# Pair products of the gated recurrence made within 64-token halves

## Chip, cores and metric

The kernel runs on one core of a Trainium2 chip. The metric is the device time of one execution in microseconds (us), smaller is better. Five engines work side by side, each through its own list of instructions in order: PE (TensorE, the matrix engine), DVE (VectorE), ACT (ScalarE), POOL (GpSimd) and SP, which issues DMAs here. They meet only at semaphores.

## What is computed

Two transformer blocks over 256 tokens of width 1024, all in float32. The change touches one part of the second block, a gated linear recurrence with 4 heads of key width 128 and value width 128:

```python
def hgrn2_mix(q, f_logit, i, g, lb, out_gain):
    ...
    def step(S, inp):
        qc, kc, vc, gc = inp
        b = jnp.cumsum(gc, axis=2)
        o_inter = jnp.einsum('bhck,bhkv->bhcv', qc * jnp.exp(b), S)
        diff = b[:, :, :, None, :] - b[:, :, None, :, :]
        decay = jnp.exp(jnp.where(causal[:, :, None], diff, -jnp.inf))
        A = jnp.einsum('bhtk,bhtsk,bhsk->bhts', qc, decay, kc)
        o = o_inter + jnp.einsum('bhts,bhsv->bhtv', A, vc)
        ...
        return S, o
```

The weight A of query t and key s (s not after t) is a sum over the 128 key channels of q, k and the product of all gates between s and t. Around it the second block has a sparse attention that picks 64 of 256 keys by index scores (heads 16 to 19 in the kernel), an attention over a memory (heads 20 to 23), and the projections and the feed-forward part, which make up most of the time.

## The kernel before

**The large products.** Every float32 weight is split by ACT into a high part (`whi`, line 817) and by DVE or POOL into the rest (`wlo`, lines 1177 and 1642), and every product is made as three matmuls (lines 470 to 472). Weights come in chunks of 256 rows through four buffers.

**The recurrence.** It is not run in steps. For each of 8 units u (head h = u // 2, tile of 128 tokens t = u % 2) the kernel makes A in blocks. The decay between key s and query t is split at a midpoint between them, so that it becomes a factor on k times a factor on q. There are 7 levels (`LEVELS`) of midpoints: level 0 splits the 128 tokens into two halves of 64, level 1 each half into quarters, and so on to neighbours; the diagonal, without decay, is the eighth. One unit goes through these steps:

1. "decay u": PE sums the log gates up to the midpoints (line 696, banks 0 and 1), and ACT takes their exponentials into `dec` (line 1119) in two pieces.
2. DVE makes `qd`, q times the factors of all 7 levels (line 1507), and for odd u `qx` (line 1512); POOL makes `kd` (line 1653), and for even u `kx`.
3. "pairs u": PE multiplies for each of the 7 levels and for the diagonal the whole 128 keys with the whole 128 queries (line 709): 8 products of 128x128, four into PSUM bank 2 and four into bank 3. For odd u one more product, "cross h" in bank 0, has the weights between the two tiles (line 713).
4. "weights u": DVE multiplies both banks by 0/1 masks that leave of each level the blocks that belong to it (line 1521, once for each bank, which also frees the bank), and sums the 8 levels into `AT` (line 1527). For odd u ACT copies the cross weights into `AT` (line 1147), which frees bank 0.
5. "hout h": PE multiplies `AT` with the values (lines 721 to 723) after the second unit of a head.

**What sets the order.** The list `MIX2`, written by hand, has all steps of this stage: gemm parts, units of the recurrence, index scores, rounds of "best" (the search of the largest index scores, lines 1485 and 1489) and attention heads ("scores", "probs", "pv"). Every engine walks through the same list and does its share of each entry, in order. So an instruction that waits holds up all later ones of its engine. The last pieces of it that matter here are

```python
("gemm", "sviq", 1), ("hout", 0), ("pairs", 2), ("decay", 3), ("sums", "sviq"),
("gemm", "mq", 0), ("turn", "iq"), *[("index", h) for h in range(4)], ("pairs", 3), ("decay", 4),
...
("gemm", "hg", 0), ("probs", 21), ("hout", 2), ("pairs", 6), ("pv", 21), ("decay", 7),
("scores", 22), ("divide", 22), ("best", 4), ("best", 5), ("turn", "sqk"), ("scores", 23), ("divide", 23),
("gemm", "hg", 1), ("pairs", 7), ("probs", 22), ("pv", 22), ("probs", 23), ("pv", 23), ("hout", 3),
```

**PSUM banks.** Banks 0 to 3 are shared by all small steps. A step claims a bank, which waits until the step before it in that bank has been read out. Banks 0 and 1 hold decays, cross, hout, index and scores; bank 2 pairs and transposed probabilities (line 544, copied out at line 908), bank 3 pairs and the attention outputs ("pv", lines 556 and 558, copied out at line 914).

Of the kernel before, what the change touches and what calls it, by code (L numbers as in the profile page):

```python
# [24 lines left out]
AX = mybir.AxisListType  # L25
# [36 lines left out]
C_HEND = C_HM + 8 * P  # L62


def constants():
# [9 lines left out]
    for n in range(LEVELS):  # L75
# [6 lines left out]
        g[:, C_HM + n * P:C_HM + (n + 1) * P] = same & late & (s <= mid)  # L82
    g[:, C_HC + 8 * P:C_HC + 9 * P] = s <= t
    g[:, C_HM + 7 * P:C_HM + 8 * P] = s == t
# [122 lines left out]
def program(nc, dram, out, known):  # L207
# [12 lines left out]
    with ctx:  # L220
# [68 lines left out]
        masked = sb("masked", [P, 8, P], where=a3)  # L289
        kx, qx = sb("kx", [P, P], where=a3), sb("qx", [P, P], where=a3)  # L290
# [147 lines left out]
        def _(pe):  # L438
# [260 lines left out]
            def hgrn_pairs(u):  # L699
# [4 lines left out]
                for b in range(2):  # L704
                    claim(2 + b, f"pairs {u}")
                    for c in range(4):
                        n, ts = 4 * b + c, slice(t * P, (t + 1) * P)
                        k, q = (kd[:, n, :], qd[:, n, :]) if n < LEVELS else (hkT[:, h, ts], hqT[:, h, ts])
                        mm = nc.tensor.matmul(X[2 + b][:, c * P:(c + 1) * P], k, q, start=True, stop=True)  # L709
                    full(mm, 2 + b, f"pairs {u}")  # L710
# [91 lines left out]
        def _(act):  # L802
# [320 lines left out]
            for kind, n, *rest in MIX2:  # L1123
# [18 lines left out]
                elif kind == "pairs" and n % 2 == 1:  # L1142
                    h = n // 2
                    act.wait_ge(*at("bank0 full", f"cross {h}"))
                    if h:
                        act.wait_ge(*at("bank1 full", f"hout {h - 1}"))
                    done(A(AT[:, 2, :], X[0][:, 0:P], ACT.Copy), "bank0 free", f"cross {h}")
# [21 lines left out]
        def _(dve):  # L1169
# [331 lines left out]
            def q_decayed(u):  # L1501
                h, t = u // 2, u % 2
                dve.wait_ge(*at("bank1 free", f"decay {u}"))
                if u:
                    dve.wait_ge(*at("bank3 full", f"pairs {u - 1}"))
# [9 lines left out]
            def weights(u):  # L1515

                h, t = u // 2, u % 2
                dve.wait_ge(*(at("weights summed", f"{u - 1}") if u else at("hgrn q", "0")))
                for b in range(2):
                    dve.wait_ge(*at(f"bank{2 + b} full", f"pairs {u}"))  # L1520
                    done(V.tensor_tensor(masked[:, 4 * b:4 * b + 4, :], X[2 + b].rearrange("p (l s) -> p l s", s=P),
                                         hgc[:, C_HM + b * 512:C_HM + (b + 1) * 512].rearrange("p (l s) -> p l s", s=P),
                                         ALU.mult), f"bank{2 + b} free", f"pairs {u}")
                dve.wait_ge(*at("bank3 free", f"pairs {u}"))
                if h:
                    dve.wait_ge(*at("bank1 full", f"hout {h - 1}"))
# [84 lines left out]
        def _(pool):  # L1611
# [23 lines left out]
            for kind, n, *rest in MIX2:  # L1635
# [10 lines left out]
                elif kind == "decay":  # L1646
# [3 lines left out]
                    if u:  # L1650
                        pool.wait_ge(*at("bank3 full", f"pairs {u - 1}"))
# [44 lines left out]
```

## Time and profile before

| what | value |
|---|---|
| three runs | 877.44, 881.36 and 881.86 us, median 881.36 |
| profiled execution, first to last instruction | 877.9 us |
| its own time beside the span | not listed apart from the three runs; one of them is 0.5 us below the span |
| instructions | 10694 |
| PE busy | 806.9 us, 92% |
| DVE busy | 550.7 us, 63% |
| ACT busy | 485.0 us, 55% |
| POOL busy | 85.5 us, 10% |
| stage of the recurrence | about 505 to 636 us of the span |

Busy shares are means over the whole program. In a row of a view "x14" says that 14 instructions are put together, and the words behind "<-" in square brackets say what ended the idle time before the first of them. A float32 matmul shows as two PE instructions. PE means the matmul itself, PEld the load of its stationary operand, 128*64 a stationary operand of 128 rows and 64 columns.

### The profile page before, as it was taken

The numbers are of one execution on the slowest core, as the hardware profiler recorded it, in microseconds if no ns is written. First come the engines' busy times: TensorE is split into PE (matmuls) and PEld (weight loads), VectorE is DVE, ScalarE is ACT, GpSimd is POOL, SyncE is SP. The second block draws the span as 40 slices with busy tenths as digits, with TensorE's granted clock in tenths as the row PEclk, the third lists the DMA queues.
The fourth block names the chain that finished last, engine by engine and source line by source line (L and its number), as shares of the span: only waits on it lengthen the run. The fifth ranks groups of instructions, "written<-read, shape, count | busy, mean of one in ns | idle before, by whom it ended". The sixth has DMA issues, their size and how long they took to land.

```text
span 877.9 us, 10694 instructions
## 1 busy us (share of the span) xinstructions
PE 806.9 (92%) x3811; PEld 650.4 (74%) x3811; DVE 550.7 (63%) x814; ACT 485.0 (55%) x739; POOL 85.5 (10%) x50
## 2 busy tenths in 40 slices
PE   4979999999799999999999798797849999999998
PEld 3767787777578888888888667665636878888886
DVE  5676565566736877777472666788773666665650
ACT  4755554666326777776254744433542677777630
POOL 0022000000000000000000047463222000000000
PEclk9999988999999999999999989898969999999999
DMA  8765153234307755545384533231001675555550
GB/s 293 296 209 173 49 162 126 96 97 143 121 24 219 238 191 190 182 151 179 134 269 164 171 95 110 70 97 49 24 25 49 198 236 179 185 181 170 194 166 24
DMA packets 70566, 130.21 MB, mean 148 GB/s; under 512 B 6558, under 2 KB 13046, under 8 KB 70142
## 3 DMA queue, kind: packets, MB, share of 16 engines
q1 hardware_dynamic: 69662, 124.90, 44.0%
q10 hardware_dynamic: 864, 4.78, 1.4%
q8 instruction: 25, 0.41, 0.2%
q14 instruction: 15, 0.12, 0.0%
HBM read 128.61 MB, written 1.05 MB: 148 GB/s over the span
## 4 chain that ended last, share of the span: by engine, by line
PE 71%; DVE 11%; ACT 8%; DMA 5%; issue 3%; POOL 1%; SPq 1%; ACTq 0%; DVEq 0%; POOLq 0%
PE acc L470 20%; PE acc L472 19%; PE acc L471 19%; DVE b_wlo L1177 3%; DMA b_raw<-in_w_in 2%; PE banks L531 2%; PE banks L696 2%; PE banks L571 2%; ACT b_whi L817 2%; PE banks L556 2%; PE banks L709 1%; DMA b_raw<-in_w_mem_kv 1%; DMA b_raw<-in_w_ffn_in 1%; PE banks L544 1%; PE banks L513 1%
## 5 line engine op out<-in xcount | busy, mean ns | idle before, releaser
L1177 DVE TENSOR_TENSOR b_wlo<-b_raw,b_whi 128x1024 fp32r<-128x1024 f32 (+3 forms) x222 | 253.4, 1179 | 103.1 <-ACT b_whi L817 101.4
L817 ACT ACTIVATE b_whi<-b_raw 128x1024 fp32r<-128x1024 f32 (+3 forms) x244 | 234.2, 1001 | 76.5 <-DMA b_raw<-in_w_in 19.1
L470 PE MATMUL acc<-b_whi,b_hhi 128*128 128x512 f32 (+3 forms) x528 | 207.7, 393 | 8.8 <-DVE b_hlo L1448 4.6
L472 PE MATMUL acc<-b_wlo,b_hhi 128*128 128x512 f32 (+3 forms) x528 | 200.4, 380 | 0.0
L471 PE MATMUL acc<-b_whi,b_hlo 128*128 128x512 f32 (+3 forms) x528 | 200.4, 380 | 0.0
L470 PEld LDWEIGHTS acc<-b_whi,b_hhi 128*128 128x128 f32 x528 | 102.3, 194 | 31.9 <-DVE b_hlo L1448 5.1
L471 PEld LDWEIGHTS acc<-b_whi,b_hlo 128*128 128x128 f32 x528 | 102.4, 194 | 18.2 <-issue 1.5
L472 PEld LDWEIGHTS acc<-b_wlo,b_hhi 128*128 128x128 f32 x528 | 102.0, 193 | 18.5
L470 PE MATMUL acc<-b_whi,b_ohi 128*128 128x512 f32 (+1 forms) x272 | 106.0, 390 | 6.1 <-DVE b_wlo L1177 2.9
L471 PE MATMUL acc<-b_whi,b_olo 128*128 128x512 f32 (+1 forms) x272 | 103.6, 381 | 0.0
L472 PE MATMUL acc<-b_wlo,b_ohi 128*128 128x512 f32 (+1 forms) x272 | 103.5, 381 | 0.0
L472 PE MATMUL acc<-b_wlo,b_ahi 128*128 128x512 f32 x176 | 69.1, 393 | 0.0
L470 PE MATMUL acc<-b_whi,b_ahi 128*128 128x512 f32 x176 | 69.1, 393 | 0.0
L471 PE MATMUL acc<-b_whi,b_alo 128*128 128x512 f32 x176 | 68.7, 390 | 0.0
L1653 POOL TENSOR_TENSOR b_kd<-b_dec,b_hkT 128x896 f32<-128x896 f32 x8 | 21.4, 2670 | 463.5 <-ACT b_dec L1119 463.5
L470 PEld LDWEIGHTS acc<-b_whi,b_ohi 128*128 128x128 f32 x272 | 51.8, 190 | 17.0 <-DVE b_wlo L1177 3.3
L472 PEld LDWEIGHTS acc<-b_wlo,b_ohi 128*128 128x128 f32 x272 | 51.7, 190 | 9.8
L471 PEld LDWEIGHTS acc<-b_whi,b_olo 128*128 128x128 f32 x272 | 51.8, 191 | 8.9
L1642 POOL TENSOR_TENSOR b_wlo<-b_raw,b_whi 128x1024 fp32r<-128x1024 f32 (+1 forms) x22 | 49.2, 2252 | 59.8 <-ACT b_whi L817 59.8
L471 PEld LDWEIGHTS acc<-b_whi,b_alo 128*128 128x128 f32 x176 | 33.1, 188 | 7.3
L472 PEld LDWEIGHTS acc<-b_wlo,b_ahi 128*128 128x128 f32 x176 | 33.1, 188 | 7.2
L470 PEld LDWEIGHTS acc<-b_whi,b_ahi 128*128 128x128 f32 x176 | 33.1, 188 | 6.9
(213 smaller groups left out, 909.5 us busy)
## 6 DMA issues: line engine op xcount, KB each, us to landing
b_raw<-in_w_in SPq DMA_DIRECT2D x64, 512.0 KB, 4.6
b_raw<-in_w_ffn_up SPq DMA_DIRECT2D x40, 512.0 KB, 4.7
b_raw<-in_w_ffn_in SPq DMA_DIRECT2D x40, 512.0 KB, 4.6
b_raw<-in_w_ffn_down SPq DMA_DIRECT2D x22, 512.0 KB, 5.6
b_raw<-in_w_ffn_out SPq DMA_DIRECT2D x22, 512.0 KB, 4.5
b_raw<-in_w_out SPq DMA_DIRECT2D x16, 512.0 KB, 3.7
b_raw<-in_w_mem_kv SPq DMA_DIRECT2D x4, 512.0 KB, 9.8
b_gates<-in_b_gate ACTq DMA_DIRECT2D x2, 1024.0 KB, 8.3
```

Source lines behind the costliest of these rows:

```text
L470: nc.tensor.matmul(o, a, wh, start=first, stop=False)
L471: nc.tensor.matmul(o, b, wh, start=False, stop=False)
L472: mm = nc.tensor.matmul(o, a, wl, start=False, stop=last)
L513: mm = nc.tensor.transpose(X[bank][:, c * S + t * P:c * S + (t + 1) * P], src[:, t, cols], ident)
L531: mm = nc.tensor.matmul(X[b][:, c0:c1], q[:, t * P:(t + 1) * P], k[:, 0:c1 - c0], start=True, stop=not fox)
L556: nc.tensor.matmul(o[:, 0:S], v[:, 0, :], pt[:, 0:S], start=True, stop=False)
L571: mm = nc.tensor.transpose(X[base + b][:, c * S + t * P:c * S + (t + 1) * P], src[:, t, (2 * b + c) * P:(2 * b + c + 1) * P], ident)
L696: full(nc.tensor.matmul(X[b][:, :], logf[:, t, h * P:(h + 1) * P], hgc[:, c:c + 512], start=True, stop=True), b, f"decay {u}")
L817: A(whi[:, n % SPLIT, 0:c["nk"], 0:c["n"]], raw[:, n % RAW, 0:c["nk"], 0:c["n"]], ACT.Copy)\
L1177: V.tensor_tensor(wlo[:, n % SPLIT, 0:c["nk"], 0:c["n"]], raw[:, n % RAW, 0:c["nk"], 0:c["n"]], whi[:, n % SPLIT, 0:c["nk"], 0:c["n"]].bit ...
L1642: G.tensor_tensor(wlo[:, low % SPLIT, 0:c["nk"], 0:c["n"]], raw[:, low % RAW, 0:c["nk"], 0:c["n"]], whi[:, low % SPLIT, 0:c["nk"], 0:c["n" ...
L1653: ins = G.tensor_tensor(kd[:, :, :], dec[:, 1 - t:8 - t, :], k.unsqueeze(1).to_broadcast([P, LEVELS, P]), ALU.mult)
```

## The change

The masks of levels 1 to 6 and of the diagonal leave nothing outside the two diagonal 64x64 blocks; level 0 alone has the block of keys 0 to 63 and queries 64 to 127, and fills it. The change makes just these blocks. Level 1 to 6 and the diagonal are two 64x64 products each, the first half of the tokens to partitions 0 to 63 and the second to partitions 64 to 127, in 7 x 64 = 448 columns of bank 2; level 0 is one 64x64 product in the last 64 columns of bank 2, on partitions 0 to 63. Bank 3 is no longer used by pairs. DVE multiplies 448 columns by masks and sums 7 levels into a new tile `near` (64 columns). ACT copies three 64x64 blocks into `AT`: level 0 out of the bank, which now is what frees bank 2, and after the sum the two blocks of `near`. The fourth block of `AT` is set to zero once. What waited for "weights summed" in "hout" now waits for "weights placed".

```diff
+def by_half(m):
+    return np.concatenate([m[:64, :64], m[64:, 64:]])
...
+        near = sb("near", [P, 64], where=a3)
...
-                for b in range(2):
-                    claim(2 + b, f"pairs {u}")
-                    for c in range(4):
-                        n, ts = 4 * b + c, slice(t * P, (t + 1) * P)
-                        k, q = (kd[:, n, :], qd[:, n, :]) if n < LEVELS else (hkT[:, h, ts], hqT[:, h, ts])
-                        mm = nc.tensor.matmul(X[2 + b][:, c * P:(c + 1) * P], k, q, start=True, stop=True)
-                    full(mm, 2 + b, f"pairs {u}")
+                claim(2, f"pairs {u}")
+                for n in range(1, LEVELS + 1):
+                    for r in range(2):
+                        own, ts = slice(64 * r, 64 * r + 64), slice(t * P + 64 * r, t * P + 64 * r + 64)
+                        k, q = (kd[:, n, own], qd[:, n, own]) if n < LEVELS else (hkT[:, h, ts], hqT[:, h, ts])
+                        nc.tensor.matmul(X[2][own, (n - 1) * 64:n * 64], k, q, start=True, stop=True)
+                full(nc.tensor.matmul(X[2][0:64, LEVELS * 64:512], kd[:, 0, 0:64], qd[:, 0, 64:P], start=True, stop=True),
+                     2, f"pairs {u}")
...
-                pe.wait_ge(*at("weights summed", f"{2 * h + 1}"))
+                pe.wait_ge(*at("weights placed", f"{2 * h + 1}"))
...
-                elif kind == "pairs" and n % 2 == 1:
-                    h = n // 2
-                    act.wait_ge(*at("bank0 full", f"cross {h}"))
+                elif kind == "pairs":
+                    h, t = n // 2, n % 2
                     if h:
                         act.wait_ge(*at("bank1 full", f"hout {h - 1}"))
-                    done(A(AT[:, 2, :], X[0][:, 0:P], ACT.Copy), "bank0 free", f"cross {h}")
+                    act.wait_ge(*at("pairs masked", f"{n}"))
+                    done(A(AT[0:64, t, 64:P], X[2][0:64, LEVELS * 64:512], ACT.Copy), "bank2 free", f"pairs {n}")
+                    if t == 1:
+                        act.wait_ge(*at("bank0 full", f"cross {h}"))
+                        done(A(AT[:, 2, :], X[0][:, 0:P], ACT.Copy), "bank0 free", f"cross {h}")
+                    act.wait_ge(*at("weights summed", f"{n}"))
+                    A(AT[0:64, t, 0:64], near[0:64, :], ACT.Copy)
+                    done(A(AT[64:P, t, 64:P], near[64:P, :], ACT.Copy), "weights placed", f"{n}")
...
-                for b in range(2):
-                    dve.wait_ge(*at(f"bank{2 + b} full", f"pairs {u}"))
-                    done(V.tensor_tensor(masked[:, 4 * b:4 * b + 4, :], X[2 + b].rearrange("p (l s) -> p l s", s=P),
-                                         hgc[:, C_HM + b * 512:C_HM + (b + 1) * 512].rearrange("p (l s) -> p l s", s=P),
-                                         ALU.mult), f"bank{2 + b} free", f"pairs {u}")
-                dve.wait_ge(*at("bank3 free", f"pairs {u}"))
-                if h:
-                    dve.wait_ge(*at("bank1 full", f"hout {h - 1}"))
-                done(V.tensor_reduce(AT[:, t, :], masked.rearrange("p l s -> p s l"), AX.X, ALU.add),
+                dve.wait_ge(*at("bank2 full", f"pairs {u}"))
+                n = LEVELS * 64
+                part = masked.rearrange("p l s -> p (l s)")[:, 0:n]
+                done(V.tensor_tensor(part, X[2][:, 0:n], hgc[:, C_HM:C_HM + n], ALU.mult), "pairs masked", f"{u}")
+                dve.wait_ge(*at("pairs masked", f"{u}"))
+                if u:
+                    dve.wait_ge(*at("weights placed", f"{u - 1}"))
+                done(V.tensor_reduce(near[:, :], part.rearrange("p (l s) -> p s l", s=64), AX.X, ALU.add),
                      "weights summed", f"{u}")
...
+            V.memset(AT[64:P, 0:2, 0:64], 0.0)
```

The table `hgc` with the masks shrinks from 2176 to 1600 columns (one DMA). Where DVE and POOL waited for "bank3 full" of the unit before, they wait for "bank2 full".

ACT around unit 2, before: between the splits of the weights and the exponentials of decay 3 nothing stands for an even unit.

```order
L817 ACTIVATE b_whi<-b_raw 128x1024 [waits s_chunk_used,s_raw_3_in]
L1119 ACTIVATE b_dec<-banks 128x512 [waits s_bank0_full,s_k_decayed,s_q_decayed]
L1119 ACTIVATE b_dec<-banks 128x512 [waits s_bank1_full]
L848 ACTIVATE b_sv<-acc,b_rs 128x256 [waits s_tile_0_summed]
L848 ACTIVATE b_spare<-acc,b_rs 128x256
```

The same place in the change:

```order
L825 ACTIVATE b_whi<-b_raw 128x1024 [waits s_chunk_used,s_raw_3_in]
L1155 ACTIVATE b_AT<-banks 64x64 [waits s_pairs_masked,s_bank1_full]
L1160 ACTIVATE b_AT<-b_near 64x64 [waits s_weights_summed]
L1161 ACTIVATE b_AT<-b_near 64x64
L1127 ACTIVATE b_dec<-banks 128x512 [waits s_bank0_full,s_k_decayed,s_q_decayed]
L1127 ACTIVATE b_dec<-banks 128x512 [waits s_bank1_full]
L856 ACTIVATE b_sv<-acc,b_rs 128x256 [waits s_tile_0_summed]
L856 ACTIVATE b_spare<-acc,b_rs 128x256
```

Three copies that wait for DVE now stand ahead of the exponentials.

PE around unit 6, before: pairs 6, then the attention output of head 21 (lines 556 and 558), then decay 7.

```order
L709 MATMUL banks<-b_qd,b_kd 128x128 [waits s_bank2_free,s_k_decayed,s_q_decayed]
L709 MATMUL banks<-b_qd,b_kd 128x128 x3
L709 MATMUL banks<-b_qd,b_kd 128x128 [waits s_bank3_free]
L709 MATMUL banks<-b_qd,b_kd 128x128 x2
L709 MATMUL banks<-b_hqT,b_hkT 128x128
L556 MATMUL banks<-b_spare,b_mv 64x256 [waits s_bank3_free,s_bank2_free]
L558 MATMUL banks<-b_spare,b_mv 64x256
L696 MATMUL banks<-b_hgc,b_logf 128x512 [waits s_bank0_free,s_log_f]
```

The same place in the change:

```order
L716 MATMUL banks<-b_qd,b_kd 64x64 [waits s_bank2_free,s_k_decayed,s_q_decayed]
L716 MATMUL banks<-b_qd,b_kd 64x64 x11
L716 MATMUL banks<-b_hqT,b_hkT 64x64 x2
L717 MATMUL banks<-b_qd,b_kd 64x64
L563 MATMUL banks<-b_spare,b_mv 64x256 [waits s_bank3_free,s_bank2_free]
L565 MATMUL banks<-b_spare,b_mv 64x256
L703 MATMUL banks<-b_hgc,b_logf 128x512 [waits s_bank0_free,s_log_f]
```

The attention output still waits for bank 3, which pairs 6 filled before and doesn't now.

## Rows read from the trace of the kernel before

**Rows 1.** Busy time by stretch: us, each engine's busy us, PE clock granted, DMA.
```profile
core 0: us, PE busy (x) PEld busy (x) DVE busy (x) ACT busy (x) POOL busy (x), PEclk, DMA share, GB/s
520.00:540.00 20.00, 19.54 (x104) 15.65 (x103) 12.72 (x12) 7.94 (x20) 13.59 (x8) 1.00 0.32 86
...
560.00:580.00 20.00, 15.34 (x69) 11.95 (x70) 17.44 (x26) 6.54 (x13) 9.60 (x4) 0.83 0.33 106
580.00:600.00 20.00, 16.63 (x83) 12.43 (x81) 16.21 (x44) 10.53 (x23) 8.53 (x5) 1.00 0.16 52
600.00:620.00 20.00, 16.13 (x61) 11.39 (x62) 15.68 (x23) 4.39 (x11) 8.29 (x3) 0.83 0.18 53
```

**Rows 2.** Chain that ended last, 505 to 640: start us, us, what.
```profile
537.26 1.73 PE banks L696 x4
539.13 0.38 issue
539.51 0.47 ACT b_sv L848
...
543.94 0.28 ACT b_ikT L1134
544.26 0.71 PE banks L672 x4
...
605.77 0.41 DVE b_xn L1588
606.18 1.21 DVE b_masked L1521 x2
607.52 0.80 PE banks L556 x2
```

**Rows 3.** DVE groups of mask and sum: busy us, mean ns, idle before.
```profile
L1527 DVE TENSOR_REDUCE b_AT<-b_masked 128x128 f32<-128x1024 f32 x8 | 15.5, 1938 | 0.3
L1521 DVE TENSOR_TENSOR b_masked<-banks,b_hgc 128x512 f32<-128x512 f32 x16 | 10.8, 687 | 4.1 <-PE banks L709 3.4
```

**Rows 4.** PE in order of time, units 1 and 4.
```profile
524.76 1.72 PE L709 MATMUL banks<-b_qd,b_kd 128*128 128x128 f32 x14
527.39 1.96 PE L696 MATMUL banks<-b_hgc,b_logf 128*128 128x512 f32 x4 [0.46 <-ACT b_AT L1147]
...
571.53 1.72 PE L709 MATMUL banks<-b_qd,b_kd 128*128 128x128 f32 x14
573.31 1.88 PE L696 MATMUL banks<-b_hgc,b_logf 128*128 128x512 f32 x4
```

**Rows 5.** PE in order of time: 128x8 products, and a change to 64 columns.
```profile
119.95 0.25 PE L470 MATMUL acc<-b_whi,b_hhi 128*128 128x8 f32 x1
120.06 0.25 PE L471 MATMUL acc<-b_whi,b_hlo 128*128 128x8 f32 x1
...
139.35 0.49 PE L544 MATMUL banks<-b_cst,b_Sm 128*128 128x128 f32 x3
139.78 0.43 PE L556 MATMUL banks<-b_PT,b_v 128*64 128x256 f32 x1
```

**Rows 6.** PEld by tile: ns min/median/max of loads with 128 and 64 columns.
```profile
L709 PEld LDWEIGHTS banks<-b_qd,b_kd x112: 186/192/338, 515.7 to 622.1; 128*128 128x128 f32 x112
...
L556 PEld LDWEIGHTS banks<-b_kd,b_sv x8: 133/136/227, 650.4 to 670.7; 128*64 128x64 f32 x8
```

**Rows 7.** PE in order of time, index scores 0 and 1 on two halves of the rows.
```profile
544.26 0.71 PE L672 MATMUL banks<-b_ikT,b_spare 64*128 64x256 f32 x4 [1.32 <-ACT b_ikT L1134]
544.80 0.39 PE L673 MATMUL banks<-b_ikT,b_spare 64*128 64x128 f32 x4
```

**Rows 8.** ACT in order of time: a 128x8 step, then decay 5.
```profile
567.43 0.21 ACT L828 ACTIVATE b_rs<-b_ms 128x8 f32<-128x8 f32 x1 [2.19 <-DVE b_ms L1251]
...
574.46 0.60 ACT L1119 ACTIVATE b_dec<-banks 128x512 f32<-128x512 f32 x1 [4.68 <-PE banks L696]
```

**Rows 9.** DVE in order of time, unit 4 and unit 6.
```profile
572.69 1.52 DVE L1521 TENSOR_TENSOR b_masked<-banks,b_hgc 128x512 f32<-128x512 f32 x2 [0.68 <-PE banks L709]
...
606.10 1.27 DVE L1521 TENSOR_TENSOR b_masked<-banks,b_hgc 128x512 f32<-128x512 f32 x2
...
612.80 1.09 DVE L1507 TENSOR_TENSOR b_qd<-b_dec,b_hqT 128x896 f32<-128x896 f32 x1 [2.75 <-ACT b_dec L1119]
```

**Rows 10.** ACT in order of time, unit 7 (and its copy of the cross weights).
```profile
624.94 0.27 ACT L1147 ACTIVATE b_AT<-banks 128x128 f32<-128x128 f32 x1
625.35 0.60 ACT L908 ACTIVATE b_spare<-banks 128x512 f32<-128x512 f32 x1
```

**Rows 11.** PE in order of time, units 6 and 7.
```profile
607.52 0.80 PE L556 MATMUL banks<-b_spare,b_mv 128*64 128x256 f32 x2 [2.90 <-DVE b_masked L1521]
...
624.66 0.66 PE L544 MATMUL banks<-b_cst,b_spare 128*128 128x128 f32 x4 [1.71 <-DVE b_masked L1521]
```

More of the change, by code:

```diff
@@ L61 @@
 C_HM = C_HC + 9 * P
-C_HEND = C_HM + 8 * P
+C_HEND = C_HM + LEVELS * 64
+def by_half(m):
+    return np.concatenate([m[:64, :64], m[64:, 64:]])
 def constants():
@@ L81, in constants @@
         same = s // (2 * half) == t // (2 * half)
-        g[:, C_HM + n * P:C_HM + (n + 1) * P] = same & late & (s <= mid)
+        if n:
+            g[:, C_HM + (n - 1) * 64:C_HM + n * 64] = by_half(same & late & (s <= mid))
     g[:, C_HC + 8 * P:C_HC + 9 * P] = s <= t
-    g[:, C_HM + 7 * P:C_HM + 8 * P] = s == t
+    g[:, C_HM + (LEVELS - 1) * 64:C_HM + LEVELS * 64] = by_half(s == t)
     freq = (500000.0 ** (-np.arange(8) * 2.0 / 16)).astype(np.float32)
@@ L1504, in q_decayed @@
                 if u:
-                    dve.wait_ge(*at("bank3 full", f"pairs {u - 1}"))
+                    dve.wait_ge(*at("bank2 full", f"pairs {u - 1}"))
                 q = hqT[:, h, t * P:(t + 1) * P]
@@ L1515, in weights @@
             def weights(u):
-                h, t = u // 2, u % 2
                 dve.wait_ge(*(at("weights summed", f"{u - 1}") if u else at("hgrn q", "0")))
-                for b in range(2):
-                    dve.wait_ge(*at(f"bank{2 + b} full", f"pairs {u}"))
-                    done(V.tensor_tensor(masked[:, 4 * b:4 * b + 4, :], X[2 + b].rearrange("p (l s) -> p l s", s=P),
-                                         hgc[:, C_HM + b * 512:C_HM + (b + 1) * 512].rearrange("p (l s) -> p l s", s=P),
-                                         ALU.mult), f"bank{2 + b} free", f"pairs {u}")
-                dve.wait_ge(*at("bank3 free", f"pairs {u}"))
-                if h:
-                    dve.wait_ge(*at("bank1 full", f"hout {h - 1}"))
-                done(V.tensor_reduce(AT[:, t, :], masked.rearrange("p l s -> p s l"), AX.X, ALU.add),
+                dve.wait_ge(*at("bank2 full", f"pairs {u}"))
[6 more added lines that the diff above has]
+                done(V.tensor_reduce(near[:, :], part.rearrange("p (l s) -> p s l", s=64), AX.X, ALU.add),
                      "weights summed", f"{u}")
@@ L1650, in _ @@
                     if u:
-                        pool.wait_ge(*at("bank3 full", f"pairs {u - 1}"))
+                        pool.wait_ge(*at("bank2 full", f"pairs {u - 1}"))
                     k = hkT[:, h, t * P:(t + 1) * P]
```

## Prediction

> **What bounds the kernel now.** I read busy time by stretch first, then the chain that ended last through the stage of the recurrence, then DVE's groups, then each engine in order of time around single units. Outside 505 to 636 us the change touches nothing but one DMA of a table, so all of the answer lies in these 130 us. There PE is busy 19.5 of 20 us up to 540 and 15 to 17 of 20 behind 560, where DVE is busy 16 to 17 of 20 [rows 1]. Neither is the bound alone: both walk one hand-written list, and the chain passes from PE to ACT and DVE and back. At unit 2 it goes PE decay, ACT copies of the projections, ACT `ikT`, PE index scores [rows 2]; at unit 6 it goes DVE copy, DVE mask, PE attention output of head 21 [rows 2]. So DVE time saved counts where DVE is on that chain, and ACT time added counts where ACT is.
>
> **What goes: DVE work.** Mask and sum cost 2 x 0.69 + 1.94 = 3.3 us a unit [rows 3]. Scaled by columns, the new ones cost 0.687 x 448 / 512 = 0.60 us and 1.938 x 448 / 1024 = 0.85 us; the sum takes out 64 columns of 7 where it took 128 of 8, which scales alike. That is 1.5 us a unit, 1.8 us less, 15 us over 8 units. Most of it isn't on the chain: in units 0 to 5 DVE waits behind it for ACT's next exponentials.
>
> **PE's burst.** Before, 16 instructions of pairs run 111 ns apart, 1.78 us (571.53 to 573.31) [rows 4]. Now there are 15 products, 30 instructions. No row has 64 stationary and 64 moving columns at once. Matmuls of 8 moving columns with a 128-column load also come 111 ns apart [rows 5], so there the load sets the distance; loads of 64 columns take 136 ns against 192, 56 ns less for 64 columns [rows 6]. One after the other, 56 ns each, 30 take 1.7 us. The change to a 64-column operand puts 0.21 us between starts where 0.11 is usual (the third of line 544 starts 139.57, line 556 at 139.78) [rows 5], twice a unit: 1.9 us. From the other side, the index scores on two halves of the rows overlap: four starts of 256 columns lie within 0.33 us, and all eight starts within 0.66 us [rows 7], where 111 ns per 128 columns gives 1.3 us. If the two halves of columns overlap fully, 30 instructions take 0.84 + 0.2 = 1.05 us. The nearest row on overlap is of rows, not columns, so I take the middle, 1.5 us, called B. The upper end is that nothing gets shorter: 30 x 0.111 + 0.2 = 3.5 us.
> The Trainium skill (TensorEngine Tiling, Key Properties) says that tiles work independently, loads and matmuls in parallel, and that a change of the tiling mode drains TensorE. By this page alone B would be near 1.05 us, and the sum 2.7 us lower than mine; rows 7 agree for tiles of rows, and no row here shows it for columns.
>
> **The new path of a unit.** Before, DVE starts on bank 2 at 1.16 us after the first matmul (572.69 against 571.53) [rows 4, 9], 0.38 us behind the start of the eighth, while the rest still runs. Now the mask waits for all 30, so it starts at B + 0.33. Then the mask takes 0.62 with its hand-over, the sum 0.86. ACT: a copy of 128x128 is 0.27 us [rows 10] and a 128x8 step is 0.21 [rows 8], so a 64x64 copy is about 0.22, with hand-over 0.25. The marks from the first matmul on:
> - bank 2 free: B + 0.33 + 0.62 + 0.3 = B + 1.25 = 2.75 us
> - cross copied, and PE's decay on its way: B + 1.63 = 3.13 us
> - ACT through with both copies of `near`, and at the exponentials: B + 0.33 + 0.62 + 0.9 + 0.5 = B + 2.35 = 3.85 us
>
> **Unit by unit.**
> - Unit 0: ACT comes to decay 1 at 3.85 us instead of some 3.0; DVE's `qd` was held up by its own sum, so only 0.35 us is left, and PE had 0.2 us of its own work to cover it. PE's shorter burst is lost in that wait. +0.2.
> - Units 1 and 3: decay u+1 needs bank 0, and waits for ACT's copy of the cross weights: 527.39 - 524.76 = 2.63 us before [rows 4], 3.13 now. Behind it PE has gemms and is on the chain. 2 x 0.5 = +1.0.
> - Units 2 and 4: ACT is at the exponentials 2.93 us after the first matmul (574.46 against 571.53) [rows 4, 8]; at 3.85 it is 0.9 late, of which 0.18 comes back since its second piece has no wait left. The chain runs through ACT here (`sv`, `ikT` for the index scores in unit 2 [rows 2], the transposed memory queries in unit 4). 2 x 0.75 = +1.5.
> - Unit 5: transposed probabilities need bank 2, free at 2.75, then decay 6 follows, 0.6 later than before. +0.6.
> - Unit 6, the one gain: PE's output of head 21 waits 2.90 us for DVE's mask to free bank 3 [rows 11], behind it decay 7, and DVE's `qd` waits 2.75 us for that [rows 9]. In the change nothing of pairs lies in bank 3, so PE runs on. What is left is DVE and ACT: mask from 606.10 [rows 9], + 0.65 + 0.86 = 607.6, copies of `near` to 608.1, ACT's copy of the output to 608.5, exponentials 1.15 to 609.65, `qd` at 609.7 instead of 612.80. From there DVE is the chain. -3.1.
> - Unit 7: probabilities of head 22 need bank 2. Before, the first mask freed it, and PE started at 624.66 [rows 11]. Now ACT must copy level 0, and ACT splits weights until 624.94 [rows 10]: PE starts at 625.25, and ACT's copy behind it comes after the copies of `near`, 0.6 late. +0.6. DVE's saving of 1.8 us is of no use, the next DVE step waits for ACT.
> - At nothing: the zeroing of a block, once, where DVE waits for ACT's splits; the table DMA, hidden by gemms before decay 0; the issue of 14 more matmul instructions a unit, inside B. Uncovered, the zeroing and the DMA cost at most some tenths of a microsecond, once.
>
> Sum: 0.2 + 1.0 + 1.5 + 0.6 - 3.1 + 0.6 = +0.8 us. Against the profiled span that is 877.9 to 878.7; the span is 3.5 us below the median of the three runs, and I add the same difference to the median: 881.4 + 0.8 = 882.2 us. B enters in six places: B = 1.05 gives -1.9 us, 1.9 gives +3.2, 3.5 gives +12.8.
>
> **Rivals.**
> 1. *Small matmuls cost as much as large ones* (slower). If issue or a fixed part and not the columns sets the 111 ns, B is 3.5 us. For it: 8 moving columns were no faster than 128 [rows 5]. Against: the loads with 64 columns are shorter [rows 6]. It decides from B = 2.2 on, where the sum passes +4.4 us. Time 894 us. Chance 0.12.
> 2. *ACT's waits hold up the splits* (slower). ACT now stands behind DVE's sum in each unit, and the weight splits behind it. If one chunk in each of units 4 to 7 came late by the 1.5 us that the sum and copies take, +6 on top: 888 us. Against: ACT is idle more than half of this stage [rows 1]. Chance 0.08.
> 3. *DVE's relief counts in full* (faster). Units 4 to 7 lie where DVE is the busiest next to PE. If the 1.8 us counted in units 4, 5 and 7 too, and the columns overlapped, it is 0.8 - 2.7 - 3 x 1.8 = -7 us: 874 us. For it: DVE busy 16 to 17 of 20 us [rows 1]. Against: the waits above. Chance 0.15.
>
> **Numbers.** My forecast, the sum with B between 1.05 and 1.9, has 0.65: about 879 to 885 us. Some 0.5% (4.4 us) is what a measurement of this kernel can tell from no change, and the three runs spread by as much. Faster by more than that 0.15, within it 0.65, slower 0.20. The range has to take in a part of both other cases: 876 to 890 us.
>
> **What would show it.** The first 64x64 matmul and the following decay in an even unit tell B: 1.5 us forecast, 3.5 in rival 1. DVE's mask should be 0.60 us and its sum 0.85. ACT's copies 0.22. PE's idle time for DVE ahead of the output of head 21, 2.9 us, must be gone, and the index scores of unit 2's turn start about 1 to 2 us later than at 544.26. If the sum stays near 1.9 us, or B is over 2.2, the forecast is wrong on the slow side; if ACT reaches the exponentials as early as before, on the fast side.

## The result, and the profile after

The change takes 883.72 us (median of 20 runs, 877.79 to 888.23) against 878.65 us for the kernel before (20 runs), a ratio of 1.0054 with the interval 1.0034 to 1.0073. The same kernel beside the experiments gave 1.0032 (1.0005 to 1.0058). So it is slower by 3 to 5 us, just around the 0.5% that a measurement can tell. The forecast was 882.2 us and "no change"; the time lies in its range. The forecast of the difference was +0.8 us, on a baseline of 881.4 us from three runs; the median of 20 runs of the kernel before is 878.65, so 2.7 us of the agreement in time are that baseline. The medians and ratios below leave out two slow runs, one of "cross copy first" (887.84 us; with it the median is 881.75) and one of "DVE, sum twice" (1155.76 us).

The head of the page of the change. PE has 112 instructions more and 3 us more of busy time, DVE 17 us less, ACT 5.5 us more.

```profile
span 884.8 us, 10939 instructions
PE 809.9 (92%) x3923; PEld 648.1 (73%) x3923; DVE 533.8 (60%) x807; ACT 490.5 (55%) x763; POOL 87.3 (10%) x50
PEclk9999988999999999999999989798959999999999
```

The groups of the new work, by line: busy us, mean ns, idle before and who ended it. They answer to [rows 3].

```profile
L1539 DVE TENSOR_REDUCE b_near<-b_masked 128x64 f32<-128x448 f32 x8 | 7.4, 924 | 0.3
L1535 DVE TENSOR_TENSOR b_masked<-banks,b_hgc 128x448 f32<-128x448 f32 x8 | 5.0, 621 | 9.6 <-PE banks L717 9.6
L1155 ACT ACTIVATE b_AT<-banks 64x64 f32<-64x64 f32 x8 | 1.7, 217 | 29.6 <-DVE b_masked L1535 29.6
L1160 ACT ACTIVATE b_AT<-b_near 64x64 f32<-64x64 f32 x8 | 2.1, 256 | 4.6 <-DVE b_near L1539 4.6
```

Mask 0.62 us (forecast 0.60), sum 0.92 (0.85), ACT's copies 0.22 and 0.26 (0.22). PE in order of time at unit 4, the place of [rows 4]:

```profile
575.39 0.92 PE L716 MATMUL banks<-b_qd,b_kd 128*64 128x64 f32 x24
576.13 0.29 PE L716 MATMUL banks<-b_hqT,b_hkT 128*64 128x64 f32 x4
576.25 0.28 PE L717 MATMUL banks<-b_qd,b_kd 128*64 128x64 f32 x2
576.46 1.98 PE L703 MATMUL banks<-b_hgc,b_logf 128*128 128x512 f32 x4
579.54 0.63 PE L520 MATMUL banks<-b_cst,b_tokA 128*128 128x128 f32 x4 [1.09 <-ACT b_dec L1127]
```

From the first product to the decay sums behind it are 576.46 - 575.39 = 1.07 us for 30 instructions: B is 1.07, not 1.5. So the burst is 0.7 us shorter than before (1.78). PE does not get to keep it: the last row has a wait of 1.09 us that the kernel before doesn't have. The chain that ended last shows why. First the kernel before, at unit 4 (start us, us, what):

```profile
571.69 1.78 PE banks L709 x16
573.48 1.72 PE banks L696 x4
575.20 0.00 issue
575.20 0.64 PE banks L513 x4
```

It stays on PE. The same stretch of the change:

```profile
575.46 0.96 PE banks L716 x28
576.64 0.64 DVE b_masked L1535
577.30 0.93 DVE b_near L1539
578.80 0.60 ACT b_dec L1127
579.54 0.64 PE banks L520 x4
```

It leaves PE, goes through DVE's mask and sum and, between 578.23 and 578.80, through ACT's two copies of `near`, and comes back by the exponentials. Before, the sum was no part of this chain: nothing but `qd` of the next unit stood behind it. The copies stand ahead of the exponentials in ACT's list, so DVE's sum now holds up PE, though it has become shorter.

**Where PE's time went**, from the start of pairs u to the start of pairs u + 1 (the last line to the output of head 3), us. "Gemm" is how much longer the gemm part in that stretch took; its 24 instructions are the same in both kernels. "Rest" is the difference without it.

| from | before | change | difference | gemm | rest | forecast |
|---|---|---|---|---|---|---|
| pairs 0 | 9.05 | 8.44 | -0.61 | | -0.61 | +0.2 |
| pairs 1 | 10.55 | 10.47 | -0.08 | | -0.08 | +0.5 |
| pairs 2 | 12.20 | 12.75 | +0.55 | | +0.55 | +0.75 |
| pairs 3 | 24.02 | 25.30 | +1.28 | +1.54 | -0.26 | +0.5 |
| pairs 4 | 11.63 | 13.81 | +2.18 | +1.70 | +0.48 | +0.75 |
| pairs 5 | 17.81 | 17.28 | -0.53 | | -0.53 | +0.6 |
| pairs 6 | 19.81 | 20.29 | +0.48 | +2.11 | -1.63 | -3.1 |
| pairs 7 | 8.58 | 7.42 | -1.16 | | -1.16 | +0.6 |
| sum | 113.65 | 115.76 | +2.11 | +5.35 | -3.24 | +0.8 |

The gemm column is a lower clock. Busy time by stretch of just these three parts (the counts take in neighbours at the edges), before:

```profile
core 0: us, PE busy (x) PEld busy (x) DVE busy (x) ACT busy (x) POOL busy (x), PEclk, DMA share, GB/s
565.20:571.50 6.30, 6.30 (x26) 5.20 (x26) 5.20 (x9) 2.35 (x5) 2.59 (x2) 0.87 0.01 5
577.60:583.20 5.60, 5.60 (x26) 4.64 (x26) 4.72 (x17) 0.81 (x3) 0.38 (x1) 1.00 0.01 3
615.20:620.80 5.60, 5.60 (x26) 4.63 (x26) 4.41 (x17) 2.00 (x6) 0.63 (x1) 1.00 0.00 0
```

and in the change:

```profile
567.50:575.40 7.90, 7.90 (x28) 6.07 (x27) 5.71 (x9) 2.38 (x5) 4.17 (x2) 0.70 0.07 18
581.90:589.20 7.30, 7.30 (x25) 5.58 (x25) 5.17 (x19) 2.85 (x6) 1.86 (x2) 0.77 0.00 0
619.10:626.80 7.70, 7.70 (x27) 5.93 (x26) 5.03 (x23) 4.22 (x12) 0.18 (x1) 0.72 0.01 2
```

PE is busy all the time in all six; the granted clock is 0.70 to 0.77 where it was 0.87 to 1.00. About half of each part runs at 1.2 GHz, the rest at 2.4. The rest column is not free of the clock either: behind pairs 6, 16 instructions of PE ahead of the gemm (scores and a turn) take 3.14 us before (612.06 to 615.20) and 4.29 in the change (614.79 to 619.08). The stage alone accounts for 2.1 us in this pair of traces; the rest of the 6.9 us between the spans lies ahead of it (decay 0 starts at 507.26 before, at 509.98 in the change) and behind it (2.1 us), where the code is the same. In the kernels below the part ahead took 503.0 to 512.6 us in one trace each, and no edit touches it. So I read stages from traces, and whole times from medians. A stage is one execution too: a second trace of the change, below, has 126.9 us for it where this one has 124.2.

### The profile page after: what moved, and what is told of

Its sections match the earlier page's. It is cut to its first block, busy times and chain, and to the rows that moved or that the text cites. A ratio compares the mean times of both kernels' runs of the same rounds, so it can differ in the third digit from the quotient of the medians.

```text
span 884.8 us, 10939 instructions
## 1 busy us (share of the span) xinstructions
PE 809.9 (92%) x3923; PEld 648.1 (73%) x3923; DVE 533.8 (60%) x807; ACT 490.5 (55%) x763; POOL 87.3 (10%) x50
## 3 DMA queue, kind: packets, MB, share of 16 engines
HBM read 128.32 MB, written 1.05 MB: 146 GB/s over the span
## 4 chain that ended last, share of the span: by engine, by line
PE 70%; DVE 11%; ACT 8%; DMA 6%; issue 3%; POOL 1%; SPq 1%; ACTq 0%; DVEq 0%; POOLq 0%
PE acc L477 20%; PE acc L479 19%; PE acc L478 19%; DVE b_wlo L1191 3%; PE banks L538 3%; ACT b_whi L825 2%; DMA b_raw<-in_w_in 2%; PE banks L578 2%; DMA b_raw<-in_w_ffn_up 2%; PE banks L563 1%; DMA b_raw<-in_w_mem_kv 1%; DMA b_raw<-in_w_ffn_in 1%; PE banks L703 1%; PE banks L520 1%; PE banks L551 1%
## 5 line engine op out<-in xcount | busy, mean ns | idle before, releaser
L477 PE MATMUL acc<-b_whi,b_hhi 128*128 128x512 f32 (+3 forms) x528 | 210.3, 398 | 13.3 <-DVE b_wlo L1191 5.7
L478 PE MATMUL acc<-b_whi,b_hlo 128*128 128x512 f32 (+3 forms) x528 | 202.8, 384 | 0.0
L479 PE MATMUL acc<-b_wlo,b_hhi 128*128 128x512 f32 (+3 forms) x528 | 202.7, 384 | 0.0
L1666 POOL TENSOR_TENSOR b_kd<-b_dec,b_hkT 128x896 f32<-128x896 f32 x8 | 24.1, 3010 | 463.3 <-ACT b_dec L1127 463.3
```

What stands on the lines that cost most here:

```text
L477: nc.tensor.matmul(o, a, wh, start=first, stop=False)
L478: nc.tensor.matmul(o, b, wh, start=False, stop=False)
L479: mm = nc.tensor.matmul(o, a, wl, start=False, stop=last)
L1666: ins = G.tensor_tensor(kd[:, :, :], dec[:, 1 - t:8 - t, :], k.unsqueeze(1).to_broadcast([P, LEVELS, P]), ALU.mult)
```

## Experiments

Twelve experiments, two of them repeats. Ratios are to the kernel before on the same chip, with 95% intervals; 12 runs of each kernel below the first two rows. The groups ran on three chips, where the kernel before has medians of 879.65, 879.72 and 880.21 us.

| kernel | median, us | ratio | stage in its trace, decay 0 to head 3's output |
|---|---|---|---|
| before | 878.65 | 1 | 122.1 |
| change | 883.72 | 1.0054 (1.0034 to 1.0073) | 124.2 |
| change again | 882.22 | 1.0032 (1.0005 to 1.0058) | 126.9 |
| pad | 881.16 | 1.0019 (0.9986 to 1.0052) | 122.4 |
| pad and warm | 878.79 | 0.9998 (0.9974 to 1.0021) | 121.0 |
| all copies on DVE | 874.57 | 0.9940 (0.9909 to 0.9972) | 115.8 |
| the same again | 874.59 | 0.9937 (0.9910 to 0.9963) | 115.7 |
| near copies on DVE | 878.73 | 0.9994 (0.9972 to 1.0017) | 122.7 |
| level 0 copy on DVE | 882.70 | 1.0027 (0.9994 to 1.0059) | 126.0 |
| cross copy first | 880.51 | 1.0009 (0.9977 to 1.0041) | 126.4 |
| DVE, bank 3 held | 878.53 | 1.0001 (0.9978 to 1.0024) | 120.9 |
| DVE, products twice | 877.92 | 0.9982 (0.9957 to 1.0007) | 123.1 |
| DVE, sum twice | 877.78 | 0.9963 (0.9933 to 0.9994) | 120.2 |
| DVE and warm | 874.58 | 0.9934 (0.9903 to 0.9964) | 115.8 |

### Is it the clock? The change again, padded, and warmed

"Change again" is the change, unaltered.

> The change once more, unaltered, to see how much of the difference between two traces is the kernel's and how much one execution's. Both theories: a ratio of about 1.005 to the kernel before. If the clock is the cause, its executions with a lower mean granted clock are the longer ones, and the stretches in which a gemm runs at the lower clock are not the same as in the first trace; the burst of pairs must again be 1.05 us and the way to the exponentials 3.4 us.

In its trace the burst at unit 4 is again 1.07 us, and ACT is at the exponentials 580.86 - 577.45 = 3.41 us behind the first product, as in the first trace. The three gemm parts are long again, but not by the same amounts:

```profile
570.50:577.40 6.90, 6.90 (x26) 5.40 (x25) 5.71 (x9) 2.44 (x5) 3.11 (x2) 0.80 0.03 12
584.40:591.20 6.80, 6.80 (x25) 5.27 (x24) 4.73 (x19) 2.79 (x6) 1.35 (x2) 0.82 0.00 0
622.70:630.80 8.10, 8.10 (x26) 6.18 (x26) 4.61 (x21) 3.72 (x8) 2.12 (x1) 0.68 0.01 2
```

They add 4.2 us to the kernel before, and the stage is 4.8 us longer, so the rest is +0.6 us here where the first trace has -3.2. What both traces show can be built on; the sum of the rest column can't.

"Pad" puts four 128x128 products of constants, which nobody reads, into bank 3, which pairs no longer use, behind each unit's pairs. They add work for PE and nothing for anyone else.

```diff
+            def pad(step, k):
+                claim(3, step)
+                for c in range(k):
+                    mm = nc.tensor.matmul(X[3][:, c % 4 * P:(c % 4 + 1) * P], hgc[:, 0:P], hgc[:, P:2 * P], start=True, stop=True)
...
+                pad(f"pad {u}", 3)
```

> The change, and behind each unit's pairs (and cross) 4 more products of 128x128 on constants into bank 3, 0.9 us of TensorE work whose result nobody reads and for which nobody waits; it lies where TensorE waits for ScalarE or is ahead of it. Theory clock (the change leaves TensorE less busy, and it is granted the lower clock more often): mean clock up, time 2 to 5 us below the change's, back near the kernel before. Theory ScalarE (its copies and waits cost the time): no gain, 0 to 3 us longer than the change, as TensorE has 7 us more to do.

"Pad and warm" adds to these 18 such products ahead of the output of head 1 and 13 ahead of pairs 6, where PE waits 5.05 and 3.01 us.

> The padded kernel, and in the two long idle stretches of TensorE (5.1 us before the output of head 1, 3.0 us before pairs 6) 18 and 13 more products of 128x128 on constants, 4.0 and 2.9 us. Theory clock: the gemms behind both stretches run at the full clock from their start, mean clock over 0.965, time 3 to 7 us below the change's, below the kernel before too. Theory ScalarE: no gain over the padded kernel.

With only more work for PE the time fell: 882.2, 881.2, 878.8 us side by side. The first two agree within their intervals, the last lies 3.4 us below the change (the intervals still overlap). The mean granted clock of the 12 runs goes 0.957, 0.962, 0.969, and is 0.964 for the kernel before beside them. The same three gemm parts in the warmed kernel:

```profile
566.30:572.00 5.70, 5.70 (x27) 4.44 (x25) 4.98 (x11) 3.01 (x6) 2.05 (x1) 1.00 0.12 46
578.60:584.20 5.60, 5.60 (x25) 4.39 (x24) 4.48 (x17) 1.14 (x5) 1.06 (x1) 1.00 0.00 1
614.60:622.00 7.40, 7.40 (x27) 5.68 (x26) 4.76 (x22) 4.22 (x12) 0.18 (x1) 0.75 0.01 2
```

Two of three are back at 5.66 us and clock 1.00 (7.87 and 7.27 in the change); the third stayed at 0.75, though 13 products stand ahead of pairs 6, some 13 us before it. "Pad" alone has 6.50, 5.66 and 7.52 us. So the four products behind pairs 4 are enough for the second part, and the first took the 18 of the warmed kernel besides.

The second part is the one that ties the clock to a wait. Four products fill PE's wait of 1.09 us behind pairs 4 (0.22 us of it are left in "pad"). Over all the traces of this document the part sorts by that wait: where it is 1.09 to 1.28 us (the change twice, cross copy first, level 0 copy on DVE) the part took 6.77 to 8.15 us, and in the ten traces without it 5.57 to 5.69.

How much of the whole loss is the clock stays open. The three parts say 5.4 and 4.2 us in the two traces of the change. The 3.4 us of the warmed kernel are no measure of it, since the kernel before has the two filled waits as well (5.06 and 3.62 us), and was not padded itself. Over the 20 runs of the change a lower mean clock goes with a longer span, a straight line through them having 5 us a hundredth (885.4 and 886.4 us at 0.946, 875.9 and 876.4 at 0.961); that is no cause yet, as the warmed version of the best kernel shows below.

### Which copy? All three, two, one, and the order

"All copies on DVE" makes the three 64x64 copies on DVE, the first between mask and sum, and leaves ACT as in the kernel before.

```diff
+                done(V.tensor_copy(AT[0:64, t, 64:P], X[2][0:64, LEVELS * 64:512]), "bank2 free", f"pairs {u}")
...
+                V.tensor_copy(AT[0:64, t, 0:64], near[0:64, :])
+                done(V.tensor_copy(AT[64:P, t, 64:P], near[64:P, :]), "weights placed", f"{u}")
```

> The change with the three 64x64 copies of each unit made by VectorE in place of ScalarE (ScalarE's share is again that of before, one copy of the cross weights for odd units). Theory ScalarE: exponentials of even units start 2.3 us behind the first matmul of pairs and not 3.4, q decayed 0.9 us sooner, time 2 to 4 us below the change's. Theory clock: within 1.5 us of the change, TensorE being as idle as in it.

It is 0.6% faster than the kernel before and 0.9% than the change: 7.7 us, where I had expected 2 to 4. The repeat agrees to 0.02 us in the median and to 0.1 us in the stage.

> The run with all three copies on VectorE again, unaltered. If its gain is real, the ratio lies between 0.991 and 0.997 and the profiled run shows a PE wait of under 1 us before the decay sums of unit 4; a ratio over 0.999 would say that the first one was luck.

Its chain at unit 4 (the repeat) is on PE alone again, and 3.0 us long where before it was 3.5 (575.20 - 571.69):

```profile
564.77 0.97 PE banks L716 x28
565.73 0.11 PE banks L717 x2
565.84 1.91 PE banks L703 x4
567.75 0.00 issue
567.76 0.64 PE banks L520 x4
```

ACT is at the exponentials 567.01 - 564.70 = 2.31 us behind the first product, where the change needs 578.80 - 575.39 = 3.41 and the kernel before 2.93 [rows 4, 8].

"Near copies on DVE" moves only the two copies of `near` (with the waits that this needs); ACT keeps the level 0 copy.

> The change with only the two copies out of near moved to VectorE; ScalarE keeps the copy of level 0, which waits for the mask but not for the sum. Theory that the wait for the sum is the cost: exponentials of even units at 2.3 us again, time within 1.5 us of 874.6. Theory that any wait of ScalarE for VectorE costs it, unit 6 above all, where the mask comes late: 2 us or more above 874.6, between that and the change.

"Level 0 copy on DVE" is the other half.

> The change with the level 0 copy alone on VectorE (between mask and sum), the two near copies stay on ScalarE. It completes the square with the runs that moved the near copies alone and all three. Queue theory (what hurts is the level 0 copy ahead of the cross copy): no PE wait over 1 us before the decay sums of unit 4, and most of the gain of the run with all three: a ratio of about 0.996 to 0.998, 876 to 879 us. If the near copies ahead of the exponentials are the larger part, the ratio stays at 1.001 to 1.003 and the exponentials of unit 1 start still at 3.3 to 3.5 us behind the pairs' first product, where all three on VectorE gave 2.3.

"Cross copy first" moves nothing, it turns ACT's order round for the odd units.

```diff
+                    if t == 1:
+                        act.wait_ge(*at("bank0 full", f"cross {h}"))
+                        done(A(AT[:, 2, :], X[0][:, 0:P], ACT.Copy), "bank0 free", f"cross {h}")
                     act.wait_ge(*at("pairs masked", f"{n}"))
                     done(A(AT[0:64, t, 64:P], X[2][0:64, LEVELS * 64:512], ACT.Copy), "bank2 free", f"pairs {n}")
```

> The change with one thing altered: for the odd units ScalarE moves the cross product out of bank 0 before it waits for the mask and moves the level 0 product. Queue theory (the cross copy stands behind a copy that waits for VectorE's mask, so bank 0 comes free late and TensorE waits before the next unit's decay sums, above all in unit 3 where the mask waits behind the index sums): the wait of TensorE before the decay sums of unit 4 falls from 1.27 us to about 0.5, those of units 2 and 6 by 0.3 to 0.5 us, and the time is 1 to 3 us below the change (881 to 883). If the copies' load on ScalarE is the cost and not their order, the time stays at that of the change within 1 us, since nothing is taken off ScalarE.

My queue theory named the level 0 copy as the larger one, and its forecast failed. With that copy alone on DVE I expected most of the gain and got little of it (1.0027, forecast 0.996 to 0.998); in the medians the near copies alone are worth more (0.9994), and both together more than the two apart (0.994). The intervals allow either half to be the larger, and also a plain sum. PE's waits in the traces say what each copy does. Four of them grew in the change (us; "again" is the second trace of the same kernel):

| PE waits before | before | change | again | cross first | level 0 on DVE | near on DVE | all on DVE |
|---|---|---|---|---|---|---|---|
| index scores of unit 2's turn | 1.32 | 1.83 | 1.83 | 1.83 | 1.83 | 1.33 | 1.33 |
| decay sums of unit 2 | 0.46 | 0.87 | 0.87 | 0.46 | 0.46 | 0.87 | 0.46 |
| decay sums of unit 4 | 0.46 | 1.27 | 0.62 | 0.52 | 0.52 | 2.59 | 0.64 |
| the turn behind decay 5 | none | 1.09 | 1.10 | 1.10 | 1.28 | none | none |
| three gemm parts, length | 17.5 | 22.8 | 21.7 | 21.6 | 20.7 | 19.3 | 17.9 |

The first of these waits and the one behind decay 5 belong to the copies of `near`, which stand ahead of the exponentials; with the level 0 copy alone on DVE both stay. ACT in order of time there, unit 4:

```profile
572.00 0.26 ACT L1159 ACTIVATE b_AT<-b_near 64x64 f32<-64x64 f32 x1 [5.30 <-DVE b_near L1541]
572.26 0.25 ACT L1160 ACTIVATE b_AT<-b_near 64x64 f32<-64x64 f32 x1
572.54 1.09 ACT L1128 ACTIVATE b_dec<-banks 128x512 f32<-128x512 f32 x2
```

and PE:

```profile
573.28 0.63 PE L520 MATMUL banks<-b_cst,b_tokA 128*128 128x128 f32 x4 [1.28 <-ACT b_dec L1128]
```

The two waits before decay sums belong to the level 0 copy: it waits for the mask, and the cross copy, which frees the bank, stands behind it on ACT. In unit 1 that costs PE 0.41 us in each of the three traces of the table with that order and nothing in the others. In unit 3 the mask waits besides behind DVE's index sums, and the size varies from one execution to the next (1.27 and 0.62 us in the same kernel). With only the near copies on DVE it is at its worst, DVE, then ACT, then PE:

```profile
544.65 0.61 DVE L1533 TENSOR_TENSOR b_masked<-banks,b_hgc 128x448 f32<-128x448 f32 x1
545.36 0.22 ACT L1156 ACTIVATE b_AT<-banks 64x64 f32<-64x64 f32 x1 [1.74 <-DVE b_masked L1533]
545.48 0.26 ACT L1159 ACTIVATE b_AT<-banks 128x128 f32<-128x128 f32 x1
```

```profile
545.88 2.90 PE L703 MATMUL banks<-b_hgc,b_logf 128*128 128x512 f32 x3 [2.59 <-ACT b_AT L1159]
```

The cross product was in its bank at 543.3 and its copy needed nothing but ACT. In "cross copy first" the added wait before unit 2's decay sums is gone, as expected, and before unit 4's there are 0.52 us. Its ratio stands 2 us below the one of the change and 4 us below the other, its stage (126.4 us) is no shorter than those of the change, and the intervals overlap, so what the order alone is worth stays open. Each half of the move takes away one kind of wait and leaves the other, and in these traces the gemm parts stay long with either; the last row of the table has 5.3 and 4.2 us over the kernel before in the change, 0.4 with all copies on DVE. Against the mean ratio of the change, 1.0043, the near copies alone give -4.3 us, the level 0 copy alone -1.4, both -9. The medians carry these three numbers; the reading by waits and clock is from one trace each, two for the change and for all copies on DVE.

The copies are not always cheap on DVE. Of the 16 copies of `near` in the repeat's trace, 12 take 0.19 us; those of units 5 and 7 take 0.63 and 2.30, 1.03 and 2.30 us. Unit 5, DVE and then POOL:

```profile
579.35 2.30 DVE L1541 COPY b_AT<-b_near 64x64 f32<-64x64 f32 x1
576.92 4.67 POOL L1656 TENSOR_TENSOR b_wlo<-b_raw,b_whi 128x1024 fp32r<-128x1024 f32 x2 [5.44 <-ACT b_whi L825]
```

In both units each of the two copies ends within 0.07 us of the end of one of POOL's two instructions.

### What were bank 3, B and DVE's time worth?

All three start from "all copies on DVE". "Bank 3 held" puts the level 0 product back into bank 3, so that pairs hold two banks as in the kernel before.

```diff
-                full(nc.tensor.matmul(X[2][0:64, LEVELS * 64:512], kd[:, 0, 0:64], qd[:, 0, 64:P], start=True, stop=True),
-                     2, f"pairs {u}")
+                full(mm, 2, f"pairs {u}")
+                claim(3, f"pairs {u}")
+                full(nc.tensor.matmul(X[3][0:64, LEVELS * 64:512], kd[:, 0, 0:64], qd[:, 0, 64:P], start=True, stop=True),
+                     3, f"pairs {u}")
```

> The kernel with the copies on VectorE, with the product of level 0 put back into bank 3, which VectorE frees by its copy. Only the output of head 21 depends on that: if the release of bank 3 is worth what the prediction said, it starts some 4 us later than without, and the time rises by 2.5 to 4 us over 874.6. If it is worth nothing because VectorE is the chain there anyway, within 1 us.

It costs 4.0 us in the medians (878.53 against 874.57) and 5.4 by the ratios (1.0001 against 0.9940), most or all of what the best version gains. PE's wait for the output of head 21 is back, at 4.07 us:

```profile
605.38 1.09 PE L563 MATMUL banks<-b_spare,b_mv 128*64 128x256 f32 x2 [4.07 <-DVE b_AT L1536]
```

"Products twice" makes the 14 products of levels 1 to 6 and the diagonal two times.

```diff
-                for n in range(1, LEVELS + 1):
+                for n in [*range(1, LEVELS + 1), *range(1, LEVELS + 1)]:
```

> The kernel with the copies on VectorE, with the 14 products of 64x64 of levels 1 to 6 and the diagonal made twice: the burst of pairs takes 2.1 us and not 1.05. Theory path: the exponentials of even units start at 3.3 us and not 2.3 behind the first matmul, six places of the sum are 1.05 us later each, time 5 to 6 us over 874.6. Theory clock alone (a shorter burst only costs clock): time unchanged or lower, mean clock up.

```profile
514.07 0.92 PE L716 MATMUL banks<-b_qd,b_kd 128*64 128x64 f32 x24 [0.23 <-issue]
...
515.72 0.28 PE L717 MATMUL banks<-b_qd,b_kd 128*64 128x64 f32 x2
515.93 1.98 PE L703 MATMUL banks<-b_hgc,b_logf 128*128 128x512 f32 x4
```

The burst is 1.86 us, 0.79 more for 28 instructions, 28 ns each. Eight times 0.79 is 6.3 us, and I expected 5 to 6; 3.4 us came out in the median and 7.3 in the stage of the one trace, 1.2 of them in the gemm parts.

"Sum twice" makes DVE's sum twice, the first time into a place that nobody reads: 0.92 us more of DVE a unit, 7.4 in all.

```diff
+                V.tensor_reduce(masked.rearrange("p l s -> p (l s)")[:, 512:576], part.rearrange("p (l s) -> p s l", s=64), AX.X, ALU.add)
                 done(V.tensor_reduce(near[:, :], part.rearrange("p (l s) -> p s l", s=64), AX.X, ALU.add),
```

> All three copies on VectorE, and the sum over the levels made twice (0.92 us more of VectorE in each of 8 units, the first into a place that nobody reads). If VectorE's own time is on the path from pairs to pairs, most of 8 x 0.92 us appears: 4 to 8 us above the run beside it without the second sum. If VectorE has room behind the mask (the next unit's decayed q waits for ScalarE's exponentials), units 0 to 5 hide it and at most 2 us appear. That also says what the 12 us of VectorE work that the change took away were worth.

3.2 us in the medians, 2.3 by the ratios, between the two answers that I had set down: three or four tenths of the DVE time added here come out in the whole. That is not the same as DVE being on the path for them. In units 1 to 3 the marks on PE don't move by more than 0.02 us from those of the version without it. All of it shows from unit 3's long stretch on, and of the 4.5 us in the stage 3.7 are longer gemm parts (7.82, 5.66 and 8.12 us), PE being busy in them. The copies of `near` also fall beside POOL's work more often, their means going from 0.35 and 0.72 to 0.82 and 1.13 us.

"DVE and warm" adds idle-filling products to the best version, 19 ahead of the output of head 1, 18 ahead of pairs 6 and 44 ahead of the probabilities of head 16.

> The kernel with the copies on VectorE, and products on constants whose result nobody reads in TensorE's three long idle stretches (19 before the output of head 1, 18 before pairs 6, 44 before the probabilities of head 16). Theory clock: the gemm behind the output of head 1 (24 instructions of each tile, 5.5 us at the full clock) takes 5.7 us and not 6.7, pairs 6 come 28 ns apart and not 56, time 2 to 5 us below that kernel's 874.6. Theory ScalarE alone: no gain, 0 to 1 us longer.

No gain (0.9934 against 0.9940 and 0.9937): the first gemm part fell from 6.74 to 5.63 us, and the third rose from 5.69 to 6.8. The mean granted clock of the 12 runs rose from 0.964 and 0.966 to 0.973 and the time stayed, so a higher mean clock is not by itself a shorter time. Filling PE's idle time gave some 3 us on top of the change and nothing here.

## Why the prediction was right, and where it was not

The time was right, and in good part by luck. The baseline was 2.7 us too high, which brought 882.2 close to the measured 883.7; the difference came out at +5.1 and +2.6 us in the medians and not at +0.8. Within the sum B was too long, and the clock, which made the kernel slower, was not in it at all: two errors in opposite directions.

- **B.** I took the middle, 1.5 us, between full overlap (1.05) and one after the other (1.9). It is 1.07. 30 instructions take 36 ns each with the changeover in it, where those of 128x128 come 111 ns apart [rows 4]. The rule of the Trainium skill (TensorEngine Tiling, Key Properties), that tiles work independently, holds here for tiles of columns as [rows 7] had it for rows. By it the sum would have been 2.7 us lower, -1.9 us in all; the rest column says -3.2 in the first trace and +0.6 in the second, so it does not decide between the two sums. Rival 1, that small products cost as much as large ones, is out.
- **What stands behind a wait.** "ACT at the exponentials at B + 2.35" was right as a form: with B = 1.07 it gives 3.42, and the trace has 3.41. So were the places: units 2 and 4 are the ones whose rest is clearly positive (+0.55 and +0.48, in the second trace +1.2 and +0.9, forecast 0.75 each), and the index scores start 546.63 - 509.98 = 36.65 us behind decay 0 (37.00 before), though I had forecast them 1 to 2 us later: the shorter bursts of units 0 to 2 gave back more than the copies took.
- **Units 1 and 3.** The wait for bank 0 was the right one: before decay 2 PE waits 0.41 us longer in both traces. But decay 2 starts 2.43 us behind the first product, 2.63 before and 3.13 in the forecast, since the burst is 0.7 us shorter. In unit 3 the level 0 copy waits for a mask that DVE makes behind its index sums, with the cross copy queued behind it: the wait before decay 4 went from 0.46 to 1.27 us in one trace and to 0.62 in the other. The prediction had the mask start at B + 0.33 everywhere.
- **Unit 6, the one gain: -3.1.** It is there. PE makes the output of head 21 at 608.03, right behind pairs 6, and DVE, in order of time, takes

```profile
611.27 0.41 DVE L1601 COPY b_xn<-banks 128x256 f32<-128x256 f32 x1
...
615.26 1.09 DVE L1521 TENSOR_TENSOR b_qd<-b_dec,b_hqT 128x896 f32<-128x896 f32 x1 [0.68 <-ACT b_dec L1127]
```

  3.99 us from the copy to `qd`, where [rows 2, 9] have 612.80 - 605.77 = 7.03: 3.04 us gained. PE starts the scores behind it 8.31 us after pairs 6 in both traces of the change and 11.09 before, 2.78 us earlier. "Bank 3 held" confirms it from the other side. By pairs 7 it was gone, to the clock: from those scores to pairs 7 the same instructions take 8.7 us before and 12.0 and 14.0 in the change.
- **Units 0, 5 and 7** each came out 0.5 to 1.2 us shorter in the first trace instead of 0.2 to 0.6 longer. B 0.43 us under my value explains a part of each. Unit 7 trades with unit 6 as well: where pairs 7 come late, the stretch behind them is shorter (20.29 and 7.43 us in the change, 15.15 and 9.90 with all copies on DVE). The rest I did not take apart.
- **The clock** has no term in the sum, and it is the largest number in the traces: +5.4 and +4.2 us in three gemm parts. It cancelled what B and the units gave. I had priced each wait at its own length; here PE's idle time in the stage went from 20.0 to 22.7 and 22.2 us, and the gemm parts grew by about twice that. For the second part the wait that goes with it is known (6.77 to 8.15 us against 5.57 to 5.69); for the first and the third it is not.
- **Rival 2** (ACT's waits hold up the splits) had the right engine and the wrong victim: the exponentials and the cross copy are seen to be held up; splits that come late were not found, and not looked for one by one. **Rival 3** (DVE's relief counts in full, 874 us) is what all copies on DVE gives, 874.6, but not for the reason given: that version's DVE is busy 544.8 us where it was 550.7 before, and at the price that "sum twice" shows those 5.9 us are worth some 2 (an estimate). Bank 3 is worth 4.0 to 5.4 us in it, and a burst longer by 0.79 us a unit costs 3.4.

## What to carry to other kernels

Before adding a small step that waits for another engine, look at what stands behind it in that engine's list: the three copies cost ACT 0.7 us a unit, but two of them put DVE's sum, and one put DVE's mask, ahead of steps that PE waits for. Give such a copy to the engine that makes what it waits for; here that turned 0.3 to 0.5% slower into 0.6% faster. And look at the clock of the gemm behind a wait of PE, not at the wait's length alone: here a part of 5.6 us took 6.8 to 8.2 behind a wait of 1.1 to 1.3 us.

## What the hardware showed

- Products on alternating 64-column tiles of PE overlap almost fully: 28 ns for each one added, 1.07 us for 30 at full clock, 1.55 us at the lower one.
- A copy of 64x64 takes DVE 0.19 us (out of `near`) or 0.21 (out of a PSUM bank) and ACT 0.26 or 0.22. Four of the 16 copies of `near` on DVE took 0.63 to 2.30 us, beside POOL's instructions of 2.3 us.
- A gemm part of 24 instructions took 5.6 us at clock 1.00 and up to 8.15 with part of it at 1.2 GHz, PE being busy throughout. The second part of the change follows 1.09 + 0.73 us of waits, where before there was 0.73. For the first part no wait close ahead tells the kernels apart (5.05 us of idle stands before it in both, and it took 6.33 us before, 7.87 and 6.87 in the change), so what sets its clock is open.
